# The first memory tile in two halves, and the second weight block held until it has landed

## The chip, the cores and the metric

The kernel runs on one core of a Trainium2 chip. The metric is the device time of one execution in microseconds (us). The kernel before takes 2175.76 us (median of 3 runs, 2175.23 to 2175.81).

## What is computed

The reference is a decoder trunk of two layers over 1024 tokens of width 1024, in float32, with 256 memory tokens beside them. Layer 0 mixes tokens by dilated window attention (12 heads of 64), layer 1 by a gated unit over chunks of 128. Each layer also attends into the memory with 4 heads, then applies an output projection, a layer norm, a SwiGLU feed-forward and another layer norm. What matters here is cut from it:

```python
mk, mv = jnp.split(mem @ w_mem_kv[i], 2, axis=-1)        # keys and values of the 256 memory tokens
h = x @ a_w_in[j]
q, k, v, qm = jnp.split(h, [DIL_WIDTH, 2 * DIL_WIDTH, 3 * DIL_WIDTH], axis=-1)
mo = memory_attention(qm, mk, mv)                        # first thing that the kernel works on
mix = dilated_attention(q, k, v)
y = jnp.concatenate([mix, mo], axis=-1) @ w_out[i]
```

## The kernel before, in words

Every float32 product is made of three matmuls on split operands (`three`, L359 to L363: high by high, low by high, high by low). A tile of 128 tokens is turned by 8 transposes on TensorE into PSUM (`turn_pe`, L1063), ScalarE copies the high part out (`turn_act`, L1075) and VectorE the rest (`turn_dve`, L1079). A block of weights (a "unit", 128 columns of a matrix, 512 KB, fetched as 512-byte pieces) is loaded into one of two raw slots by `load` (L235 to L243) from the SyncE queue, and GpSimd splits it into high and low (`split`, L318 and L321). `load` of unit u waits until unit u - 2 has been split (`split_done`); units 0 and 1 wait for nothing. A projection on TensorE (`proj_pe`) waits until its unit has been split.

The opening of the kernel, which is all that the change touches:

- SyncE's queue loads units in the order 0 (memory keys, from `w_mem_kv`), 1 (memory queries, from `a_w_in`), 2 (memory values), 3 (keys of the second pair of memory heads), 4, and so on.
- ScalarE's queue issues, one after the other, the identity matrix (64 KB), memory tile 0, memory tile 1 (512 KB each, 4 KB pieces), and then x in five DMAs: tile 0, tile 1, tiles 2 and 3, 4 and 5, 6 and 7 (4 MB in all). Only then does ScalarE begin to compute.
- TensorE, in its program's order: turn memory tiles 0 and 1, x tile 0, wait for the low part of memory tile 0, x tile 1, wait for the low part of memory tile 1, the key projection of unit 0 (24 matmuls of 256 columns), turn x tiles 2 to 5, the query projection of unit 1 (24 matmuls of 512 columns), turn x tiles 6 and 7, the first part of the value projection of unit 2, and then the attention stream, in which the projections of later units are interleaved. Where one of these waits, everything behind it on TensorE waits too.
- GpSimd splits the units in their order.

SyncE's DMAs are queue q1 in the profile, ScalarE's are q10. Both are served by the same 16 DMA engines.

Of the kernel before, what the change touches and what calls it, by code (L numbers as in the profile page):

```python
# [25 lines left out]
D = 1024  # L26
# [3 lines left out]
KT = D // P  # L30
# [53 lines left out]
def build(nc, a, out):  # L84
    base = -(-nc.sbuf_base // 64) * 64

    def at(name, shape, dt, off):
        return nc.alloc_sbuf_tensor_at(name, shape, dt, offset=base + off)
# [3 lines left out]
    def sem(name):  # L92
        if name not in sems:
            sems[name] = nc.alloc_semaphore(name)
        return sems[name]
# [22 lines left out]
    memraw = at("memraw", [P, 2, D], F32, A_MV + 16 * KB)  # L118
# [107 lines left out]
    def bank(b, n=512, off=0):  # L226
        return ps[:, 512 * b + off:512 * b + off + n]


    def cols(w, c0):  # L230

        return w[:, bass.ds(c0, P)].rearrange("(k p) c -> p k c", p=P)


    def load(sp, u, src):  # L235
        if not (isinstance(u, int) and u < RS):
            sp.wait_ge(split_done, u - RS + 1)
        slot = load.turn % RS
        load.turn += 1
        dst = raw[:, slot, :]  # L240
        if len(src.shape) == 3:
            dst = dst.rearrange("p (k c) -> p k c", c=P)
        sp.dma_start(dst, src).then_inc(raw_landed[slot], 16)  # L243
# [19 lines left out]
    def letters(p):  # L263

        return "qkv" if p >= NMP else "kqv"
# [200 lines left out]
    def at_(name, value=None):  # L466
        s = sem(f"att_{name}")
        return s if value is None else (s, value)
# [147 lines left out]
    def proj_pe(pe, what, g, h, k0, k1):  # L616

        u = weight_unit(g, what, h)
        n = proj_cols(g, what)
        if k0 == 0:  # L620
            pe.wait_ge(split_done, u + 1)
            if bank_user(what, g, h):
                pe.wait_ge(*evacuated(*bank_user(what, g, h)))
            if (what, g, h) == ("q", 0, 1):
                pe.wait_ge(*gi("xt_low", NT))
            if (what, g, h) == ("q", 8, 1):
                pe.wait_ge(*gf[0]("xt_low", 2 * KT))
        for k in range(k0, k1):
            wh, wl = wtile(slot_of(u), k)
            if n == M:  # L630
                xh, xl = memTh[:, k, :], memTl[:, k, :]
            else:
                xh, xl = XTh[:, k, h * 512:h * 512 + 512], XTl[:, k, h * 512:h * 512 + 512]
            mm = three(bank(proj_bank(g, what, h), n), wh, wl, xh, xl, k == 0, k == KT - 1)
        if k1 == KT:
            mm.then_inc(at_(f"{what}_proj"), 1)

    def v_turn_pe(pe, g, h):
        r = rank(g, "v", h)
        pe.wait_ge(*at_("v_copied", r + 1))  # L640
        for t in range(proj_cols(g, "v") // P):
            mm = nc.tensor.transpose(bank(proj_bank(g, "v", h), P, t * P), buf(g).vT[:, t * P:(t + 1) * P], ident[:, :])
        mm.then_inc(at_("v_turned"), 1)
# [410 lines left out]
            if L == 0 and j == len(seq):  # L1054
                out_dve(dve, 0)

    def turn_pe(pe, g, t, src, nk=KT, bb=0, after=None):

        if t >= 2:
            pe.wait_ge(*g("xt_low", t - 1 if after is None else after))  # L1060
        b = bb + 2 * (t % 2)
        for k in range(nk):
            mm = nc.tensor.transpose(bank(b + k // 4, P, (k % 4) * P), src(k), ident[:, :])  # L1063
        mm.then_inc(g("xt_turned"), 1)

    def columns(x):
        return lambda k: x[:, k * P:(k + 1) * P]
# [71 lines left out]
    def row_turn(pe, g, j, c):  # L1139
        h, k = j // KT, j % KT  # L1140
        if k == 0:
            pe.wait_ge(*g("normed", 4 * h + 4))
        if j == KT or (j == 0 and g is gf[0]):
            pe.wait_ge(*g("added", first_unit(g, c) + 8 * (h + 1 if g is gf[0] else 2) + g.credit))
        b, before = row_bank(g, j)
        if before is not None:
            pe.wait_ge(*row_read(g, before))
        for i in range(4):
            mm = nc.tensor.transpose(bank(b, P, i * P), XR[:, 4 * h + i, k * P:(k + 1) * P], ident[:, :])  # L1149
        mm.then_inc(g("row_turned"), 1)  # L1150
# [11 lines left out]
    def row_read(g, j):  # L1162

        return g("odd_high" if j % 2 else "even_high", j // 2 + 1)
# [216 lines left out]
    gm = [Names("memory", {"xt_turned": 2, "xt_high": 2, "xt_low": 2}, L) for L in range(2)]  # L1381
# [114 lines left out]
    def turn_memory_pe(pe, t):  # L1496

        if t == 0:
            pe.wait_ge(sem("mem_landed1"), 32)
            pe.wait_ge(*gf[0]("gated", 4 * NCONV + 2))  # L1500
        else:
            pe.wait_ge(*gf[0]("added", UNITS_OF_FFN - 2 + gf[0].credit))
        turn_pe(pe, gm[1], t, columns(memraw[:, 1 - t, :]), bb=1 + t)
# [213 lines left out]
    def pair_pe(pe, L, p, first=False, second=False):  # L1717
        tile_pe(pe, L, p, 0, first, second)
        tile_pe(pe, L, p, 1, first)
# [762 lines left out]
    def x_banks(t):  # L2482

        return X_BANK[t] - 2 * (t % 2)
# [6 lines left out]
    def _(sp):  # L2491
        w = [a["a_w_in"][0], a["b_w_in"][0]]

        def mem_units():
            for p in range(NMP):
                src = {"q": cols(w[0], 3 * DIL_W + p * P), "k": cols(a["w_mem_kv"][0], p * P),
                       "v": cols(a["w_mem_kv"][0], MEM_W + p * P)}
                for j in range(3):
                    load(sp, 3 * p + j, src[letters(p)[j]])

        def second_units():
# [192 lines left out]
    @block.tensor  # L2694
    def _(pe):
        pe.wait_ge(sem("const_landed"), 16)
        def turn_x(t):
            if t in X_FROM:
                pe.wait_ge(sem(f"x_landed{X_FROM.index(t)}"), 16)
            turn_pe(pe, gi, t, columns(XR[:, t, :]), bb=x_banks(t), after=X_AFTER[t])  # L2700

        def ready_first(g, i):
            if (g, i) == (0, 0):
                pe.wait_ge(*gi("xt_low", 7))
        for t in range(2):
            pe.wait_ge(sem(f"mem_tile{t}"), 16)
            turn_pe(pe, gm[0], t, columns(memraw[:, t, :]), bb=4)
        turn_x(0)
        pe.wait_ge(*gm[0]("xt_low", 1))
        turn_x(1)  # L2710
        pe.wait_ge(*gm[0]("xt_low", 2))
        proj_pe(pe, "k", 0, 0, 0, KT)
        for t in range(2, 6):
            if t == 4:
                pe.wait_ge(*at_("k_low", 2))
            turn_x(t)
        pe.wait_ge(*gi("xt_low", 4))
        proj_pe(pe, "q", 0, 0, 0, KT)
        turn_x(6)
        turn_x(7)  # L2720
        proj_pe(pe, "v", 0, 0, 0, 3)
        for L in range(2):
            if L == 0:
                attention_pe(pe, 0, ready_first)
            else:
                pe.wait_ge(*gf[0]("gated", 4 * NCONV + 2))
                proj_pe(pe, "q", 9, 0, 0, 3)
                turn_memory_pe(pe, 1)
                proj_pe(pe, "q", 9, 0, 3, 6)
                for j in (KT, KT + 1):  # L2730
                    row_turn(pe, gf[0], j, LAST)
                proj_pe(pe, "q", 9, 0, 6, KT)
                pe.wait_ge(*gm[1]("xt_low", 2))
                for j in (KT + 2, KT + 3):
                    row_turn(pe, gf[0], j, LAST)
                proj_pe(pe, "k", 8, 0, 0, KT)
                for j in (KT + 4, KT + 5):
                    row_turn(pe, gf[0], j, LAST)
                proj_pe(pe, "v", 8, 0, 0, KT)
                for j in (KT + 6, KT + 7):  # L2740
                    row_turn(pe, gf[0], j, LAST)
                v_turn_pe(pe, 8, 0)

                def ready(g, i):
                    if (g, i) == (8, 0):
                        pe.wait_ge(*row_read(gf[0], 2 * KT - 2))
                        pe.wait_ge(*row_read(gf[0], 2 * KT - 1))
                attention_pe(pe, 1, ready)
                sgu_pe(pe)

            for c in range(len(OUT_PARTS[L])):
                out_pe(pe, L, c, range(3 - L, NT) if c == 0 else range(NT))
            ffn_pe(pe, L, 0, True, False)
            pair_pe(pe, L, 0, first=True)
            pair_pe(pe, L, 1, second=True)
            with pe.Fori(2, NP - 1) as p:
                pair_pe(pe, L, p)
            pair_pe(pe, L, NP - 1)
            ffn_pe(pe, L, 1, False, True)

    @block.scalar
    def _(act):
        act.dma_start(ident[:, :], a["c_ident"]).then_inc(sem("const_landed"), 16)
        mem = a["mem"][0].rearrange("(t p) d -> p t d", p=P)
        for t in range(2):
            act.dma_start(memraw[:, t, :], mem[:, t, :]).then_inc(sem(f"mem_tile{t}"), 16)
        for i in range(X_PARTS):
            act.dma_start(XR[:, X_FROM[i]:X_FROM[i + 1], :],
                          a["x"][0, P * X_FROM[i]:P * X_FROM[i + 1], :].rearrange("(t p) d -> p t d", p=P)
# [209 lines left out]
```

## Time and profile before

| | |
|---|---|
| median of 3 runs | 2175.76 us |
| span of the profiled execution | 2173.8 us |
| TensorE matmul busy | 2143.0 us (99%) |
| VectorE busy | 1343.5 us (62%) |
| GpSimd busy | 1301.1 us (60%) |
| ScalarE busy | 929.9 us (43%) |
| granted TensorE clock, mean | 0.997 |

The span runs from the first to the last instruction of the profiled execution. No separate time of that execution is given; the median of the runs is 1.96 us above its span, which is what lies around it. In a timeline row the columns are the start and the duration in us, the engine (SPq and ACTq are the DMA-issuing sides of SyncE and ScalarE, PE is TensorE, DVE VectorE, POOL GpSimd), the line, the operation, what it writes and reads, the shape and the count, and in square brackets the idle time before it with what ended it.

### The profile page before, as it was taken

How to read it: one execution, taken by the hardware profiler on the slowest of the kernel's cores; microseconds unless marked ns; L12 is line 12 of the kernel's file. 1: busy time of each engine (PE TensorE's matmuls, PEld its weight loads, DVE VectorE, ACT ScalarE, POOL GpSimd, SP SyncE). 2: the span in 40 equal slices, each digit the busy share in tenths (PEclk: the TensorE clock that was granted, in tenths of full speed). 3: DMA queues.
4: the chain of work that ended last, by engine and by line, in shares of the span. 5: the costliest groups of instructions: out<-in, count | busy, mean ns of one | idle time of the engine just before them, and what ended most of it. 6: DMA issues, size and time to landing. Idle time of an engine off the chain costs nothing.

```text
span 2173.8 us, 32211 instructions
## 1 busy us (share of the span) xinstructions
PE 2143.0 (99%) x10960; PEld 1822.5 (84%) x10960; DVE 1343.5 (62%) x2447; ACT 929.9 (43%) x1751; POOL 1301.1 (60%) x863
## 2 busy tenths in 40 slices
PE   8999999999999999999999999999999999999997
PEld 7888888888888888888888899988878888888885
DVE  5655565655875555566547747657866555555567
ACT  5655555632533343443324753213444333333323
POOL 5221222374498777777773793424698777777764
PEclk9999999999999999999999999999999999999998
DMA  5211111142012111111131311201012111111111
GB/s 176 74 53 46 58 49 59 44 136 59 20 59 59 58 51 55 54 51 55 46 96 49 102 48 47 78 22 57 20 59 68 55 57 54 58 58 58 54 62 79
DMA packets 164701, 132.64 MB, mean 61 GB/s; under 512 B 12656, under 2 KB 148464, under 8 KB 164592
## 3 DMA queue, kind: packets, MB, share of 16 engines
q1 hardware_dynamic: 149568, 115.36, 17.6%
q10 hardware_dynamic: 15024, 15.83, 2.5%
q8 instruction: 68, 1.11, 0.2%
q14 instruction: 41, 0.34, 0.0%
HBM read 122.78 MB, written 4.19 MB: 58 GB/s over the span
## 4 chain that ended last, share of the span: by engine, by line
PE 91%; DVE 4%; POOL 3%; issue 1%; ACT 1%; DMA 0%; ACTq 0%; DVEq 0%; POOLq 0%
PE ps L361 27%; PE ps L363 27%; PE ps L362 27%; PE ps L716 3%; PE ps L744 2%; PE ps L745 2%; PE ps L703 2%; PE ps L704 1%; POOL Rl L1896 1%; PE ps L1149 1%; POOL XR L1333 1%; PE ps L1063 1%; DVE V L2418 1%; POOL raw L1918 0%; DVE T2l L1606 0%
## 5 line engine op out<-in xcount | busy, mean ns | idle before, releaser
L2102 DVE TENSOR_TENSOR XR<-XR,ps 128x512 f32<-128x512 f32 x504 | 338.8, 686 | 215.4 <-PE ps L363 215.4
L318 POOL TENSOR_TENSOR Wh<-raw,zcol 128x1024 fp32r<-128x1024 f32 x76 | 144.7, 1904 | 466.6 <-PE ps L363 389.5
L1896 POOL TENSOR_TENSOR Rl<-raw,Rh 128x512 fp32r<-128x512 f32 x216 | 285.6, 1324 | 121.4 <-ACT Rh L1740 118.9
L361 PE MATMUL ps<-XTh,Wh 128*128 128x512 f32 x608 | 248.6, 409 | 0.5 <-DVE bQl L922 0.4
L363 PE MATMUL ps<-XTh,Wl 128*128 128x512 f32 x608 | 238.2, 392 | 0.0
L362 PE MATMUL ps<-XTl,Wh 128*128 128x512 f32 x608 | 237.8, 391 | 0.0
L361 PE MATMUL ps<-XTh,Rh 128*128 128x512 f32 x576 | 224.3, 389 | 3.3 <-POOL Rl L1896 3.3
L362 PE MATMUL ps<-XTl,Rh 128*128 128x512 f32 x576 | 224.1, 389 | 0.0
L363 PE MATMUL ps<-XTh,Rl 128*128 128x512 f32 x576 | 224.1, 389 | 0.0
L1740 ACT ACTIVATE Rh<-raw 128x512 fp32r<-128x512 f32 x216 | 135.8, 630 | 167.7 <-PE ps L363 143.6
L361 PE MATMUL ps<-Wh,XTh 128*128 128x256 f32 (+1 forms) x576 | 192.0, 333 | 0.0
L363 PE MATMUL ps<-Wh,XTl 128*128 128x256 f32 (+1 forms) x576 | 190.2, 330 | 0.0
L362 PE MATMUL ps<-Wl,XTh 128*128 128x256 f32 (+1 forms) x576 | 190.2, 330 | 0.0
L321 POOL TENSOR_TENSOR Wl<-raw,Wh 128x1024 fp32r<-128x1024 f32 x76 | 183.7, 2418 | 6.0
L1941 POOL TENSOR_TENSOR DRl<-rows,DRh 128x512 fp32r<-128x512 f32 x108 | 140.6, 1303 | 72.5 <-ACT DRh L1811 72.5
L1811 ACT ACTIVATE DRh<-rows 128x512 fp32r<-128x512 f32 x108 | 68.2, 631 | 174.0 <-PE ps L363 174.0
L363 PEld LDWEIGHTS ps<-XTh,Wl 128*128 128x128 f32 x608 | 114.1, 188 | 25.5
L361 PEld LDWEIGHTS ps<-XTh,Rh 128*128 128x128 f32 x576 | 108.1, 188 | 26.6 <-POOL Rl L1896 4.2
L361 PEld LDWEIGHTS ps<-XTh,Wh 128*128 128x128 f32 x608 | 114.4, 188 | 16.4 <-issue 0.6
L362 PEld LDWEIGHTS ps<-XTl,Wh 128*128 128x128 f32 x608 | 114.8, 189 | 15.1
L363 PEld LDWEIGHTS ps<-XTh,Rl 128*128 128x128 f32 x576 | 108.1, 188 | 22.5
L362 PEld LDWEIGHTS ps<-XTl,Rh 128*128 128x128 f32 x576 | 108.1, 188 | 22.4
(302 smaller groups left out, 5572.4 us busy)
## 6 DMA issues: line engine op xcount, KB each, us to landing
raw<-in_w_up SPq DMA_DIRECT2D x44, 512.0 KB, 3.8
raw<-in_w_gate SPq DMA_DIRECT2D x72, 256.0 KB, 2.9
rows<-in_w_down SPq DMA_DIRECT2D x36, 512.0 KB, 3.7
raw<-in_a_w_in SPq DMA_DIRECT2D x20, 512.0 KB, 3.8
raw<-in_w_out SPq DMA_DIRECT2D x16, 512.0 KB, 3.7
raw<-in_b_w_in SPq DMA_DIRECT2D x15, 512.0 KB, 3.8
B<-in_c_bias SPq DMA_DIRECT2D x12, 512.0 KB, 3.7
raw<-in_w_mem_kv SPq DMA_DIRECT2D x8, 512.0 KB, 3.9
```

What stands on the lines that cost most here:

```text
L318: nc.gpsimd.tensor_tensor(high, raw[:, turn, :], zcol[:, 0:1].to_broadcast([P, UNIT]), ALU.add).then_inc(high_done, 1)
L321: nc.gpsimd.tensor_tensor(low, raw[:, turn, :], high.bitcast(F32), ALU.subtract).then_inc(split_done, 1)
L361: nc.tensor.matmul(dst, wh, xh, start=first, stop=False, skip_group_check=onto)
L362: nc.tensor.matmul(dst, wh, xl, start=False, stop=False, skip_group_check=onto)
L363: return nc.tensor.matmul(dst, wl, xh, start=False, stop=last, skip_group_check=onto)
L703: nc.tensor.matmul(bank(u % SU, nb), bf.Qh[:, hd, qt * P:(qt + 1) * P], K, start=True, stop=False)
L716: mm = nc.tensor.transpose(bank(4 + gi % 2, P, x * P), probs_of(g, 2 * s + ab, (lo + k) * P, (lo + k + 1) * P), ident[:, :])
L1740: nc.scalar.activation(Rh[(w - 1) % 4][:, :], source(w), ACT.Copy).then_inc(g("high"), 1)
L1811: nc.scalar.activation(DRh[:, (d - 1) % 2, :], right_source(d), ACT.Copy).then_inc(g("right_high"), 1)
L1896: nc.gpsimd.tensor_tensor(Rl[(w - 1) % 4][:, :], source(w), Rh[(w - 1) % 4][:, :].bitcast(F32), ALU.subtract).then_inc(gs[L]("low"), 1)
L1941: nc.gpsimd.tensor_tensor(DRl[:, (d - 1) % 2, :], right_source(d), DRh[:, (d - 1) % 2, :].bitcast(F32), ALU.subtract).then_inc(gs[L]("righ ...
L2102: nc.vector.tensor_tensor(x, x, bank(4 + i), ALU.add).then_inc(gf[L]("added"), 1)
```

## The change

Memory tile 0 is fetched as two DMAs of 128 rows by 512 columns (2 KB pieces, 256 KB each). The first half has a semaphore of its own, `mem_half0`; the second counts on `mem_tile0`. TensorE waits for the first half ahead of its first four transposes and for the second half ahead of the other four. SyncE waits for `mem_tile0` before it issues the load of unit 1; units 2 and later stand behind that in its program.

```diff
-    def turn_pe(pe, g, t, src, nk=KT, bb=0, after=None):
+    def turn_pe(pe, g, t, src, nk=KT, bb=0, after=None, half=None):
...
         for k in range(nk):
+            if half and k == KT // 2:
+                half()
             mm = nc.tensor.transpose(bank(b + k // 4, P, (k % 4) * P), src(k), ident[:, :])
...
                 for j in range(3):
+                    if (p, j) == (0, 1):
+                        sp.wait_ge(sem("mem_tile0"), 16)
                     load(sp, 3 * p + j, src[letters(p)[j]])
...
         for t in range(2):
-            pe.wait_ge(sem(f"mem_tile{t}"), 16)
-            turn_pe(pe, gm[0], t, columns(memraw[:, t, :]), bb=4)
+            if t == 0:
+                pe.wait_ge(sem("mem_half0"), 16)
+            else:
+                pe.wait_ge(sem(f"mem_tile{t}"), 16)
+            turn_pe(pe, gm[0], t, columns(memraw[:, t, :]), bb=4,
+                    half=lambda t=t: pe.wait_ge(sem(f"mem_tile{t}"), 16) if t == 0 else None)
...
         for t in range(2):
-            act.dma_start(memraw[:, t, :], mem[:, t, :]).then_inc(sem(f"mem_tile{t}"), 16)
+            for h in range(2) if t == 0 else (None,):
+                cs = slice(0, D) if h is None else slice(h * 512, h * 512 + 512)
+                act.dma_start(memraw[:, t, cs], mem[:, t, cs]).then_inc(
+                    sem("mem_half0") if (t, h) == (0, 0) else sem(f"mem_tile{t}"), 16)
```

## Rows read from the trace of the kernel before

**Rows 1.** The chain of waits that ended last, by engine, share of the span.
```profile
PE 91%; DVE 4%; POOL 3%; issue 1%; ACT 1%; DMA 0%; ACTq 0%; DVEq 0%; POOLq 0%
```
**Rows 2.** TensorE's waits, whole span: total us, times, longest us.
```profile
PE ps L1063 <- DMA memraw<-in_mem: 7.6, 1, 7.6
PE ps L361 <- POOL Rl L1896: 3.3, 2, 1.7
```
**Rows 3.** Timeline of the first 41 us, all engines.
```profile
0.82 0.43 SPq L243 DMA_DIRECT2D raw<-in_w_mem_kv  x1
...
1.31 1.24 ACTq L2766 DMA_DIRECT2D memraw<-in_mem  x2
1.32 0.58 SPq L243 DMA_DIRECT2D raw<-in_a_w_in  x1
2.57 2.48 ACTq L2768 DMA_DIRECT2D XR<-in_x  x5
...
5.19 1.89 POOL L318 TENSOR_TENSOR Wh<-raw,zcol 128x1024 fp32r<-128x1024 f32 x1 [4.28 <-DMA raw<-in_w_mem_kv]
...
7.63 3.65 PE L1063 MATMUL ps<-ident,memraw 128*128 128x128 f32 x16 [7.63 <-DMA memraw<-in_mem]
9.54 6.65 SPq L243 DMA_DIRECT2D raw<-in_w_mem_kv  x2
...
11.42 1.90 POOL L318 TENSOR_TENSOR Wh<-raw,zcol 128x1024 fp32r<-128x1024 f32 x1 [1.90 <-DMA raw<-in_a_w_in]
...
12.38 1.23 DVE L1079 TENSOR_TENSOR memTl<-ps,memTh 128x1024 fp32r<-128x1024 f32 x1 [0.48 <-ACT memTh L1075]
13.39 2.40 POOL L321 TENSOR_TENSOR Wl<-raw,Wh 128x1024 fp32r<-128x1024 f32 x1
...
13.66 0.39 PE L361 MATMUL ps<-memTh,Wh 128*128 128x256 f32 x1 [0.53 <-DVE memTl L1079]
...
20.05 1.09 PE L1063 MATMUL ps<-ident,XR 128*128 128x128 f32 x8 [0.63 <-DVE XTl L1079]
...
21.18 0.50 PE L361 MATMUL ps<-XTh,Wh 128*128 128x512 f32 x1
...
21.54 1.89 POOL L318 TENSOR_TENSOR Wh<-raw,zcol 128x1024 fp32r<-128x1024 f32 x1 [5.74 <-DMA raw<-in_w_mem_kv]
...
28.42 0.36 PE L361 MATMUL ps<-memTh,Wh 128*128 128x256 f32 x1
...
40.48 0.28 PE L361 MATMUL ps<-memTh,Wh 128*128 128x256 f32 x1
```
**Rows 4.** DMAs issued from 1.3 to 1.4 us: KB, us from issue to landing.
```profile
memraw<-in_mem ACTq DMA_DIRECT2D x1, 512.0 KB, 6.2
raw<-in_a_w_in SPq DMA_DIRECT2D x1, 512.0 KB, 10.0
```
**Rows 5.** DMA issued from 9 to 10 us.
```profile
raw<-in_w_mem_kv SPq DMA_DIRECT2D x1, 512.0 KB, 11.9
```
**Rows 6.** DMA queues, 0 to 3.5 us: packets, MB, share of 16 engines.
```profile
q1 hardware_dynamic: 491, 0.25, 24.4%
q10 hardware_dynamic: 126, 0.06, 6.1%
```
**Rows 7.** DMA queues, 4 to 5 us (q10 has no row there).
```profile
q1 hardware_dynamic: 655, 0.33, 116.0%
```
**Rows 8.** DMA queues, 5 to 6 us.
```profile
q10 hardware_dynamic: 66, 0.27, 78.9%
q1 hardware_dynamic: 151, 0.08, 31.2%
```
**Rows 9.** DMA queues, 13.2 to 20.1 us.
```profile
q10 hardware_dynamic: 616, 2.34, 86.5%
q1 hardware_dynamic: 662, 0.34, 17.1%
```
**Rows 10.** DMA queues, 20.1 to 20.8 us.
```profile
q1 hardware_dynamic: 463, 0.23, 116.8%
```

## The prediction, as made before the run

> **What bounds the kernel now.** I read the chain of waits first. The reader is to see that TensorE holds 91% of it and DMA nothing that counts [rows 1]: the time is TensorE's program, end to end, so a change matters by what it adds to or takes from TensorE's idle time. TensorE's own waits say where that is: one of 7.6 us at the start, for memory tile 0, and after it little; the next group is two waits, 3.3 us together [rows 2]. After the opening nothing has enough slack to give back a delay of TensorE, and a gain there would likewise last to the end.
>
> So I read the timeline of the opening, then the DMA landings and queues. TensorE starts at 7.63 on memory tile 0, runs 16 transposes, and begins the key projection at 13.66, released by VectorE's low part of memory tile 1 (12.38 + 1.23 = 13.61). The query projection (unit 1) starts at 21.18, right behind the last x transposes (20.05 + 1.09 = 21.14). Unit 1 landed at 1.32 + 10.0 = 11.32 [rows 4], GpSimd split it from 11.42 to 13.39 + 2.40 = 15.79 [rows 3]. So its slack is 21.18 - 15.79 = 5.4 us. That slack is what the change spends.
>
> **Why memory tile 0 is late today.** It is issued at 1.31, as unit 1 is, and lands 6.2 us later, at 7.5 [rows 3, 4]. Up to 3.5 us the queues share: q1 moved 491 packets, q10 126 (the identity) [rows 6]. From 4 to 5 us q10 has no packet at all while q1 moves 655 [rows 7]; only from 5 to 6 do 4 KB packets come on q10 [rows 8]. 491 + 655 is over the 1024 packets of unit 0, so unit 1 ran in that gap, ahead of tile 0, though q10's request was as old. I read it thus: requests of both queues are turned into descriptors in the order of their issue, one after the other. The same shows in unit 2: issued at 9.54 when q1 was almost empty, it took 11.9 us [rows 5], having the x DMAs (issued 2.57 to 5.05, [rows 3]) before it.
>
> **Part 1, unit 1 held back: what the front gains.** Without unit 1 in the way, tile 0 should start right behind the identity: about 3.6 instead of 5.0 us, 1.4 earlier. At that time unit 0 has 1024 - 491 = 533 packets left at 3.5, some 480 at 3.6, which is like the some 570 of unit 1 (2048 - 491 - 655, less what passed from 3.5 to 4) that stood beside tile 0 before. So tile 0 takes its 2.5 us as before (5.0 to 7.5) and lands at about 6.1, tile 1 about 1.4 earlier too, near 7.8 (16 transposes without a break from 7.63 put its arrival before now at no later than 9.5). The chain 16 transposes, ScalarE, VectorE then ends near 12.0, against 13.6.
>
> But the key projection also needs unit 0 split. Unit 0's last 480 packets now stand beside tile 0 and tile 1, where before they were alone. Unit 1's rest needed from 5.0 to 11.3 in that position, 6.3 us; so unit 0 lands at 3.6 + 6.3 = 9.9 at the latest, instead of about 5.1. At the earliest: tile 0 now comes in 256 packets of 2 KB, and if the engines take the queues in turn, 256 of unit 0 pass beside them until 6.1 less 0.6 for the landing; the other 224 pass at 96 per us [rows 9] in 2.3 us, and it lands at 8.4. I take 9.0, between the two. A split takes 15.79 - 11.42 = 4.37 us [rows 3], so unit 0 is ready at 13.4 (12.8 to 14.3), and the key projection starts there: 0.3 us earlier than 13.66, bounds 0.9 earlier and 0.7 later. The gain of 1.6 on the tile is mostly turned into a wait for unit 0. From there to the query projection is 21.18 - 13.66 = 7.5 us of work, so that x is ready at 20.9 (20.3 to 21.9).
>
> **Part 2, what holding back costs.** SyncE waits until about 6.1, then issues unit 1. Queued behind it in SyncE's program are unit 2 and all others; their own condition (the split of unit 0) comes at 13.4, later than that. By 6.1 all x DMAs are issued, the last at about 5.05 + 0.6 for the extra issue of a half. Unit 1 therefore takes the place that unit 2 has today: behind 4 MB of x. Unit 2's landing was 9.54 + 11.9 = 21.44. It consists of sharing (13.2 to 20.1: 662 packets in 6.9 us, 96 per us, beside x) [rows 9] and of a burst once x is over (463 in 0.7 us, 660 per us) [rows 10]. x ends 1.4 us earlier, as it starts earlier and the bytes beside it are nearly the same. So unit 1 lands at 21.44 - 1.4 = 20.0, is picked up 0.1 later (21.54 against 21.44), and is split at 20.1 + 4.4 = 24.5. The query projection starts at 24.5 instead of 21.18: **+3.3 us**.
>
> Bounds. If unit 1 isn't held behind x but flows from 1.6 us after its issue, 7.7, at 96 per us, it needs 10.7 us: 18.4 and 0.6 for the landing, 19.0, so +2.3. If tile 0 doesn't start earlier but x follows without unit 1's rest beside it (570 packets of 512 B, 0.29 MB at 2.68 MB in 6.9 us [rows 9], 0.75 us), unit 1 lands at 20.7: +4.0.
>
> **Part 3, the rest.** The first half lets TensorE start near 5.0 instead of 7.6; this is before a wait (13.4) that starts no earlier for it: nothing. One added wait on TensorE, one added issue of 0.6 us on ScalarE (1.24 for two): ScalarE is idle until its first copy at 9.6: nothing; without that cover 0.6. Unit 2 follows unit 1 by some 1.7 us (21.7), is split behind it, 24.5 to 28.9; its projection stood at 28.42 and now comes at 28.42 + 3.3 = 31.7. Unit 3 is issued at 24.5, used at 40.48 + 3.3: covered. Later units follow TensorE. Turning x 6 and 7 and the rest stay behind the query projection, so nothing regains the 3.3.
>
> **Sum.** 2173.8 + 3.3 = 2177.1 of span, with 1.96 around it: 2179.1, which is the median plus 3.3.
>
> **The clock.** The 16 transposes after the idle start took 3.65 us, 0.228 each; 8 of x at 20.05 took 1.09, 0.136 each [rows 3]. The one is the 1.2 GHz level, the other 2.4. The new idle time before the query projection is 24.5 - 20.9 = 3.6 us, longer than any after the start (1.7, [rows 2]). Should the clock fall in it, the next work loses about what the start did: 16 transposes at full pitch take some 1.9 us, so 3.65 - 1.9 = 1.7 us. The Trainium skill ("TensorE: Matmul & The Clock Gate", Part 1) says that the clock of an idle TensorE is halved and restored only after sustained activity. The trace agrees at the start; no row shows a gap as long as this one.
>
> **Rivals.**
> - The clock falls in the gap: 3.3 + 1.7 = +5.0, 2180.8. For it: the slow start. Against: the gap is half as long as that at the start, and 1.7 us gaps left no mark in the mean clock of 0.997.
> - Unit 1 arrives in time and unit 0 isn't slowed: faster. The place is the key projection, released by tile 1 at 12.0 instead of 13.66: -1.6, 2174.2. It decides if unit 1 is split by 21.18 - 1.6 = 19.6, so landed by 15.2; from 7.7 that asks for 137 packets per us against 96 measured beside x. And unit 0 would have to land by 7.6.
> - Unit 0 late, unit 1 in time: the key projection at 14.3, +0.7, 2176.5. Same objection.
> - The change doesn't do what it says: q10's gap from 4 to 5 us is a latency of ScalarE's queue, not unit 1. Then tile 0 still lands near 7, and unit 1 at 20.7: +4.0, 2179.8, within the main case's bounds.
>
> **How the numbers follow.** Main case 0.70 (2178.1 to 2179.8, of it 0.10 the last rival); falling clock 0.13; gain 0.09; unit 0 alone 0.03; nothing measurable either way 0.05. 0.2% is 4.35 us, about what tells a change from none: the line for slower is 2180.1. Slower is the falling clock and a sliver of the main case, 0.15; faster would need 2171.4, which no case gives: 0.01; the rest, 0.84, is within. The range leaves out the full gain and what is beyond the falling clock: 2176.6 to 2181.0.
>
> **What would show it.** Tile 0's first packets from 3.6 us; TensorE's first transpose near 5; unit 0's split from about 9 instead of 5.2; GpSimd's second split starting near 20.1 instead of 11.42; TensorE idle over 3 us before the 128x512 matmuls of L361, released by GpSimd (L321). If that second split starts before 16, I am wrong in the main step; if the matmuls behind the gap run at half pitch, the clock rival holds.

## The result, and the profile after

The changed kernel takes 2181.41 us (median of 8 runs, 2180.56 to 2181.87); the kernel before takes 2175.73 us beside it (8 runs, 2175.23 to 2176.35). The ratio is 1.0026, with an interval of 1.0016 to 1.0036: +5.7 us, slower. The prediction said 2179.1 with a range up to 2181.0; the time lies outside the range by 0.4 us. The span grew by 6.0 us, from 2173.8 to 2179.8.

TensorE's waits over the whole span (total us, times, longest) answer to [rows 2]:

```profile
PE ps L1065 <- DMA memraw<-in_mem: 6.3, 1, 6.3
PE ps L361 <- POOL Wl L321: 5.0, 1, 5.0
PE ps L361 <- POOL Rl L1898: 3.3, 2, 1.6
```

The wait for memory tile 0 became 1.3 us shorter, and one of 5.0 us, for GpSimd's split of unit 1, is new. The timeline of the opening answers to [rows 3]; line numbers behind the edits are higher, by 2 at first and by more for the DMAs of ScalarE:

```profile
0.82 0.43 SPq L243 DMA_DIRECT2D raw<-in_w_mem_kv  x1
...
1.30 1.57 ACTq L2776 DMA_DIRECT2D memraw<-in_mem  x3
2.90 2.78 ACTq L2779 DMA_DIRECT2D XR<-in_x  x5
5.25 1.89 POOL L318 TENSOR_TENSOR Wh<-raw,zcol 128x1024 fp32r<-128x1024 f32 x1 [4.34 <-DMA raw<-in_w_mem_kv]
...
6.26 3.68 PE L1065 MATMUL ps<-ident,memraw 128*128 128x128 f32 x16 [6.26 <-DMA memraw<-in_mem]
6.78 0.38 SPq L243 DMA_DIRECT2D raw<-in_a_w_in  x1
...
12.31 0.38 PE L361 MATMUL ps<-memTh,Wh 128*128 128x256 f32 x1 [0.49 <-DVE memTl L1081]
...
18.70 1.09 PE L1065 MATMUL ps<-ident,XR 128*128 128x128 f32 x8 [0.63 <-DVE XTl L1081]
...
20.38 1.89 POOL L318 TENSOR_TENSOR Wh<-raw,zcol 128x1024 fp32r<-128x1024 f32 x1 [10.80 <-DMA raw<-in_a_w_in]
...
22.35 2.35 POOL L321 TENSOR_TENSOR Wl<-raw,Wh 128x1024 fp32r<-128x1024 f32 x1
...
24.84 0.77 PE L361 MATMUL ps<-XTh,Wh 128*128 128x512 f32 x1 [5.05 <-POOL Wl L321]
25.40 0.63 PE L362 MATMUL ps<-XTl,Wh 128*128 128x512 f32 x1
...
29.67 0.61 PE L363 MATMUL ps<-XTh,Wl 128*128 128x512 f32 x1
30.09 0.42 PE L361 MATMUL ps<-XTh,Wh 128*128 128x512 f32 x1
30.35 0.39 PE L362 MATMUL ps<-XTl,Wh 128*128 128x512 f32 x1
...
32.85 1.91 PE L1065 MATMUL ps<-ident,XR 128*128 128x128 f32 x16
```

The 6 us can be read off it in three pieces.

1. The front gained 1.35 us: the key projection starts at 12.31 instead of 13.66, and the last x tile ahead of the query projection is turned at 18.70 + 1.09 = 19.79 instead of 21.14.
2. From there TensorE sits idle for 5.05 us, to 24.84. Unit 1 is picked up by GpSimd at 20.38 instead of 11.42. With the gain of piece 1 the query projection is 24.84 - 21.18 = 3.66 us later.
3. Its first 12 matmuls stand 0.427 us apart (25.40 to 29.67 is ten steps), the last 12 about 0.226. That is the 1.2 GHz level and then the 2.4 GHz one. The projection takes 32.85 - 24.84 = 8.01 us. Before, it took 26.75 - 21.18 = 5.57 us, since TensorE turned x tile 6 at:

```profile
26.75 1.91 PE L1063 MATMUL ps<-ident,XR 128*128 128x128 f32 x16
```

So the slow clock costs 2.4 us. The profile's record of the clock says the same. In these rows stand the stretch, its length, TensorE's busy time and matmuls in it, the granted clock as a share of 2.4 GHz, and what the DMA engines did:

```profile
22.50:23.00 0.50, 0.00 (x0) 1.00 0.00 0
23.00:23.50 0.50, 0.00 (x0) 0.81 0.00 0
29.00:30.00 1.00, 1.00 (x4) 0.50 0.00 0
30.00:31.00 1.00, 1.00 (x5) 0.93 0.65 138
```

The clock fell between 23.0 and 23.5, while TensorE was idle, and rose after 30.0, in the middle of the projection.

3.66 + 2.4 is 6.1, which is the growth of the span within 0.1 us. Nothing later gives any of it back.

### The profile page after: what moved, and what is told of

It reads as the page before. It is cut to its first block, busy times and chain, and to the rows that moved or that the text cites. A ratio compares the mean times of both kernels' runs of the same rounds, so it can differ in the third digit from the quotient of the medians.

```text
span 2179.8 us, 32212 instructions
## 1 busy us (share of the span) xinstructions
PE 2145.5 (98%) x10960; PEld 1824.4 (84%) x10960; DVE 1343.1 (62%) x2447; ACT 929.3 (43%) x1751; POOL 1300.0 (60%) x863
## 3 DMA queue, kind: packets, MB, share of 16 engines
HBM read 122.78 MB, written 4.19 MB: 58 GB/s over the span
## 4 chain that ended last, share of the span: by engine, by line
PE 91%; DVE 4%; POOL 3%; issue 1%; DMA 1%; ACT 1%; ACTq 0%; DVEq 0%; POOLq 0%
PE ps L361 27%; PE ps L363 27%; PE ps L362 26%; PE ps L716 3%; PE ps L744 2%; PE ps L745 2%; PE ps L703 2%; PE ps L704 1%; POOL Rl L1898 1%; PE ps L1151 1%; POOL XR L1335 1%; DMA raw<-in_a_w_in 1%; DVE V L2420 1%; POOL raw L1920 0%; DVE T2l L1608 0%
## 5 line engine op out<-in xcount | busy, mean ns | idle before, releaser
L361 PE MATMUL ps<-XTh,Wh 128*128 128x512 f32 x608 | 249.7, 411 | 5.5 <-POOL Wl L321 5.0
L361 PE MATMUL ps<-XTh,Rh 128*128 128x512 f32 x576 | 224.4, 390 | 3.3 <-POOL Rl L1898 3.3
L361 PE MATMUL ps<-Wh,XTh 128*128 128x256 f32 (+1 forms) x576 | 192.1, 333 | 0.0
L361 PEld LDWEIGHTS ps<-XTh,Wh 128*128 128x128 f32 x608 | 115.2, 189 | 21.6 <-DVE XTl L1081 5.3
L361 PEld LDWEIGHTS ps<-XTh,Rh 128*128 128x128 f32 x576 | 108.1, 188 | 26.4 <-POOL Rl L1898 4.1
```

The source lines that it names most:

```text
L361: nc.tensor.matmul(dst, wh, xh, start=first, stop=False, skip_group_check=onto)
```

## The experiments

Every time is compared with runs of the kernel before on the same chip, whose median was 2175.79 us for e1 to e4, 2175.74 for e5, e6, e8 and e9, and 2175.91 for f1 to f4. "Query start" is the start of the first 128x512 matmul of L361: 21.18 before, 24.84 after.

### e1 and e2: each part alone

e1 is the changed kernel without SyncE's wait; e2 is the kernel before with that wait alone.

```diff
--- e1, against the changed kernel
-                    if (p, j) == (0, 1):
-                        sp.wait_ge(sem("mem_tile0"), 16)
--- e2, against the kernel before
+                    if (p, j) == (0, 1):
+                        sp.wait_ge(sem("mem_tile0"), 16)
```

> The changed kernel with SyncE's wait taken out: only tile 0 in halves. My theory (the whole loss is unit 1 behind x and the slow clock after the idle time): unit 1 lands near 11.4 and is split by 16, no idle time before the query projection, which starts at 21.2 +- 0.3; the time is that of before within 0.5 us. If the half tiles themselves cost (smaller packets, one more issue, one more wait on TensorE), the key projection starts later than 13.66 by that cost, and up to 1 us of the 5.7 is theirs.

> The kernel before with SyncE's wait alone, tile 0 whole. My theory: unit 1 is issued near 6.8 to 7.2, lands at 20 to 20.6, the query projection starts near 25, its first 12 or so matmuls stand at 0.43 us pitch instead of 0.23, and the time is that of the changed kernel within 0.7 us (+5 to +6.4). If the halves carry a part of the loss, it is less than +5.

e1: 2175.99 us (+0.2; ratio 1.0000, 0.9991 to 1.0009), query start 21.34. e2: 2181.34 us (+5.6; ratio 1.0025, 1.0015 to 1.0034), query start 24.56, and TensorE turns x tile 6 at 32.74, as after (32.85). Timeline of e2:

```profile
6.67 0.38 SPq L243 DMA_DIRECT2D raw<-in_a_w_in  x1
6.79 3.34 PE L1063 MATMUL ps<-ident,memraw 128*128 128x128 f32 x16 [6.79 <-DMA memraw<-in_mem]
...
20.09 1.90 POOL L318 TENSOR_TENSOR Wh<-raw,zcol 128x1024 fp32r<-128x1024 f32 x1 [10.25 <-DMA raw<-in_a_w_in]
...
32.74 1.91 PE L1063 MATMUL ps<-ident,XR 128*128 128x128 f32 x16
```

The wait makes both the front's gain (in e2 TensorE is ready for the query projection at 19.98, 1.2 us earlier than before) and the whole loss. The halves alone make no difference that can be measured.

### e3 and e8: is it the idle time that lowers the clock?

Transposes of the identity, written to a free PSUM bank and read by nobody, are put ahead of the query projection: 34 in e3, 12 in e8.

```diff
+        for _ in range(34):          # 12 in e8
+            nc.tensor.transpose(bank(3, P), ident[:, :], ident[:, :])
         proj_pe(pe, "q", 0, 0, 0, KT)
```

> The changed kernel with 34 extra transposes of the identity into an unused PSUM bank right ahead of the query projection: they fill 4 us of the 5.05 us idle time and are read by nobody. My theory, that the idle time drops TensorE to its 1.2 GHz level: the query projection still starts at 24.8 but all of its matmuls stand at 0.23 us pitch; against before +3.7 instead of +5.7 to +6.1, so 2179.4. The rival, that the slow matmuls come from what runs beside them (GpSimd splitting units 1 and 2, the DMAs), expects 0.43 us pitch for some 12 of them all the same and +6.

> The changed kernel with 12 extra transposes ahead of the query projection, which are done 1.4 us after the last of x and leave about 3.6 us idle, the gap that my prediction had. My theory has no firm value: if a gap of 3.6 us is enough for the clock to fall, the time is that of the changed kernel (+5.7) and the pitch 0.43 for some 10 to 12 matmuls; if not, +3.7 as with the gap filled. Either tells whether the prediction's main case was wrong about the clock even with its own gap.

e3: 2180.07 us (+4.3; ratio 1.0020, 1.0011 to 1.0029). The extra transposes and the matmuls of L361 in e3's query projection (line, count, busy us, mean ns, idle before):

```profile
L2727 PE MATMUL ps<-ident 128*128 128x128 f32 x34 | 3.9, 274 | 0.0
L361 PE MATMUL ps<-XTh,Wh 128*128 128x512 f32 x8 | 3.2, 406 | 0.7 <-POOL Wl L321 0.7
```

and after, by the same view:

```profile
L361 PE MATMUL ps<-XTh,Wh 128*128 128x512 f32 x8 | 4.2, 529 | 5.0 <-POOL Wl L321 5.0
```

Query start is 24.71, x tile 6 is turned at 30.33: 5.62 us for the projection instead of 8.01, at the same place, beside the same splits on GpSimd and the same DMAs. The granted clock stays at 1.00 through the gap and the projection. Filling the gap took the slow matmuls away; the rival that they come from the work beside them falls.

The median gained 1.3 us rather than 2.4, and stands 0.6 above the 2179.4 expected. A part of that is the execution: the profiled one of e3 took 2179.57, 0.5 us below its median. The rest is open. Executions also differ in what the slow clock costs: in the profiles with a gap of 4.3 us or more, the projection took 7.13 us (e9), 7.16 (e5), 8.01 (after), 8.12 (e6) and 8.18 (e2), which is 1.6 to 2.6 us over the 5.57 of before.

e8: 2180.66 us (+4.9; ratio 1.0024, 1.0014 to 1.0035), with runs from 2179.67 to 2182.62, the widest spread here. In its profiled execution the gap was 3.2 us, not the 3.6 aimed at, and the clock held (granted 1.00 throughout):

```profile
L361 PE MATMUL ps<-XTh,Wh 128*128 128x512 f32 x8 | 3.2, 406 | 3.2 <-POOL Wl L321 3.2
```

Most of its loss is then the late start. The second half of memory tile 0 landed late in this execution, so unit 1 was issued at 7.58 and the query start is 25.33, 4.15 us later than before. x tile 6 is turned 4.2 us later, and the span is 5.1 us longer. Where the last 0.9 us arise was not found. The slowest run, 2182.62, has a mean granted clock of 0.996, as seven of the eight runs after the change have; the other eight runs of e8 have 0.997. So the clock may well have fallen in that one.

Of gaps seen in profiles, 3.2 us left the clock at 2.4 GHz, and 4.3 (e9), 4.6 (e2), 4.9 (e5, e6) and 5.05 us (after) dropped it to 1.2 GHz. But the length of the gap does not tell when it falls. TensorE's last work before the gap ended at 19.79 after, and the clock fell between 23.0 and 23.5. In e5 it ended at 20.01, and the clock was down from 21.5 on; in e9 it ended at 20.52, and the clock was still up at 25.0, with the projection begun. The rows of e5 and of e9:

```profile
21.50:22.00 0.50, 0.00 (x0) 0.52 0.00 0
```
```profile
24.50:25.00 0.50, 0.16 (x1) 1.00 0.00 0
25.00:26.00 1.00, 1.00 (x3) 0.51 0.15 26
```

So it fell from 1.5 to 4.5 us after the last work, and e8's one profile does not show that a gap of 3.6 us is safe.

### e4: unit 1 ahead of all of x

```diff
                     if (p, j) == (0, 1):
-                        sp.wait_ge(sem("mem_tile0"), 16)
+                        load.turn += 1
+                        continue
...
+        act.dma_start(raw[:, 1, :].rearrange("p (k c) -> p k c", c=P),
+                      cols(a["a_w_in"][0], 3 * DIL_W)).then_inc(raw_landed[1], 16)
         for i in range(X_PARTS):
```

> The changed kernel, but unit 1 is issued by ScalarE between memory tile 1 and x instead of by SyncE after tile 0 has landed. My theory, that what delays unit 1 is x standing ahead of it: it lands by 11 to 12, is split by 16, there is no idle time before the query projection, and the front's gain stays: key projection at 12.3, query projection at 19.8, time 1.0 to 1.4 below before. The rival, that a late unit 1 is late by being kept off the engines until tile 0 is through, and is as late from any queue, expects it after 15.5 and no gain.

2176.98 us (+1.2; ratio 1.0004, 0.9995 to 1.0013). Unit 1 was there at 10.66, as expected. The expected gain did not come:

```profile
10.66 1.89 POOL L318 TENSOR_TENSOR Wh<-raw,zcol 128x1024 fp32r<-128x1024 f32 x1 [0.86 <-DMA raw<-in_a_w_in]
11.90 3.67 PE L1065 MATMUL ps<-ident,XR 128*128 128x128 f32 x16 [1.07 <-DMA XR<-in_x]
...
23.11 0.50 PE L361 MATMUL ps<-XTh,Wh 128*128 128x512 f32 x1
```

x tile 0 now comes behind unit 1, at 11.9, after an idle time of 1.07 us. TensorE turns it ahead of the key projection, and the 16 transposes took 3.67 us, the pitch of the slow level; the gaps before them are a likely reason, but this was not tried. The key projection started at 15.2 and the query projection 1.9 us late, from x and not from unit 1, which had been split by 15.0.

### e5 and e6: is unit 1 late because it stands behind x?

This was the prediction's reason. e5 issues unit 1 earlier, at the identity's landing; e6 issues x tiles 4 to 7 after it.

```diff
--- e5
-                        sp.wait_ge(sem("mem_tile0"), 16)
+                        sp.wait_ge(sem("const_landed"), 16)
--- e6
-        for i in range(X_PARTS):
+        def fetch_x(i):
...
-        for t in range(2):
-            turn_act(act, gm[0], t, bb=4, high=memTh)
+        for i in range(3):
+            fetch_x(i)
+        turn_act(act, gm[0], 0, bb=4, high=memTh)
+        fetch_x(3)
+        fetch_x(4)
+        turn_act(act, gm[0], 1, bb=4, high=memTh)
```

> The changed kernel, but SyncE holds unit 1 only until the identity has landed (4.2 us) instead of tile 0's second half (6.8). At 4.2 x tiles 0, 1 and 2 to 3 are issued, x tiles 4 to 7 are not or just being issued. My theory, that descriptors of both queues are made in the order of issue: unit 1 then stands ahead of 1 to 2 MB of x, starts near 6 to 9 and lands between 13 and 17; if by 15.3, the query projection starts at 19.8 and the time is 1.3 below before; at 17 it starts at 21.5, about even. The rival, that the queues share fairly from the moment of issue, expects unit 1 from 5.8 on at some 96 packets per us, landing at 16 to 17.

> The changed kernel with SyncE's wait kept, but ScalarE issues x tiles 4 to 7 (2 MB) only after its first copy of memory tile 0 (about 9.3 us) instead of before 5.7. My theory: unit 1, issued at 6.8, has only x tiles 0 to 3 ahead of it, starts before 9 and lands near 12 to 14, so that the query projection isn't kept waiting; time 1.0 to 1.4 below before, unless x tiles 4 and 5 (then landing near 15 to 17) come late for their turn at 17.2. The rival, that the wait itself is what costs, expects unit 1 near 20 as before.

e5: 2181.72 us (+6.0; ratio 1.0027, 1.0017 to 1.0038). e6: 2181.37 us (+5.6; ratio 1.0027, 1.0017 to 1.0036). Both expectations of my theory failed. In e5 unit 1 was issued 2.6 us earlier than after, in e6 the second half of x at 8.35 instead of before 5.7, and unit 1 was picked up at 20.47 and 20.40, against 20.38 after. The rival in e5's expectation, even sharing from the issue on and a landing at 16 to 17, failed too. The DMA rows (KB, us to landing) of after, e5 and e6 in turn:

```profile
raw<-in_a_w_in SPq DMA_DIRECT2D x1, 512.0 KB, 13.5
```
```profile
raw<-in_a_w_in SPq DMA_DIRECT2D x1, 512.0 KB, 16.2
```
```profile
raw<-in_a_w_in SPq DMA_DIRECT2D x1, 512.0 KB, 13.4
```

In e5 unit 1 did begin earlier, with 9 packets between 7 and 8 us, where after there are none up to 10. It gained nothing by it. The queues show why. After, 11 to 18 us (packets, MB, share of 16 engines):

```profile
q10 hardware_dynamic: 635, 2.47, 88.1%
q1 hardware_dynamic: 637, 0.33, 15.7%
```

e5, 8 to 18 us:

```profile
q10 hardware_dynamic: 913, 3.48, 88.1%
q1 hardware_dynamic: 892, 0.46, 15.7%
```

The two queues pass the same number of packets, within 3%. One packet is 4 KB for x and 512 bytes for a weight unit, so unit 1 gets about a ninth of the bytes. Its 1024 packets outnumber those that x has left when unit 1 begins (x has 1024 in all), so it can't end before x does.

### f2: the same unit in 4 KB pieces

```diff
-                    load(sp, 3 * p + j, src[letters(p)[j]])
+                    load(sp, 3 * p + j, a["w_out"][0][0:P, :] if (p, j) == (0, 1) else src[letters(p)[j]])
```

> The changed kernel, but unit 1's load reads 128 whole rows of another matrix (w_out) in its place: the same 512 KB at the same point of the queue in pieces of 4 KB instead of 512 bytes. It leaves out the true query weights of the first pair of memory heads. The last two experiments moved unit 1's issue from 6.8 to 4.2 us, and 2 MB of x from ahead of it to behind it, and it landed at 20.3 to 20.4 all the same. My theory now: beside x a queue gets one packet for each of the other's, whatever their size, so 1024 small packets take as long as x lasts. Then 128 packets of 4 KB start near 10.8 as before and are through in some 1.5 us: unit 1 lands at 12 to 13.5, the query projection starts at 19.8 without a wait, and the time is 1.0 to 1.4 below before. The old theory, unit 1 stands behind x in the order of issue, has it land near 20 here too, and +5.7.

2174.56 us (-1.35; ratio 0.9994, 0.9985 to 1.0004; runs 2174.29 to 2175.09 against 2175.27 to 2176.54). Unit 1's DMA and the timeline:

```profile
raw<-in_w_out SPq DMA_DIRECT2D x1, 512.0 KB, 7.4
```
```profile
7.06 0.35 SPq L243 DMA_DIRECT2D raw<-in_w_out  x1
...
14.56 1.90 POOL L318 TENSOR_TENSOR Wh<-raw,zcol 128x1024 fp32r<-128x1024 f32 x1 [4.84 <-DMA raw<-in_w_out]
...
20.01 0.50 PE L361 MATMUL ps<-XTh,Wh 128*128 128x512 f32 x1
```

The queues of f2 from 12 to 13 us:

```profile
q10 hardware_dynamic: 51, 0.21, 50.8%
q1 hardware_dynamic: 51, 0.21, 50.7%
```

The wait is as after, the issue is at 7.06, and what differs is the size of the pieces and, with it, the place in memory that they are read from. The unit lands 7.4 us after its issue instead of 13.5, no wait stands before the query projection, and the front's gain is left alone: 21.18 - 20.01 = 1.2 us, and 1.35 in the medians. The interval holds 1, so the gain is not shown by it, though every run of f2 lies below every run of before; that the loss is gone is clear. Unit 1 landed at 14.5 and not at 12 to 13.5 as I expected. 51 packets per us to each queue make 2.5 us for 128, not 1.5; what else it took was not looked into.

This is shown: the loss of the change is gone when unit 1 comes in 4 KB pieces at the same point of the queue. No run reads small pieces from the other place or large ones from the old, but the packets speak for the piece size: one to one in both cases, with 51 to 51 here and 635 to 637 after.

### e9: tile 0 ahead of the identity

```diff
-        act.dma_start(ident[:, :], a["c_ident"]).then_inc(sem("const_landed"), 16)
...
+            if t == 0:
+                act.dma_start(ident[:, :], a["c_ident"]).then_inc(sem("const_landed"), 16)
```

> The changed kernel with tile 0's two halves issued ahead of the identity on ScalarE's queue. It tests the step of the prediction that failed, that unit 0's packets would stand beside tile 0's and land at 8.4 to 9.9. If descriptors are made in the order of issue and the engines then take the queues in turn, tile 0's packets start near 3.3, with over 500 of unit 0 left, unit 0 lands after 7 instead of 5.2, and the key projection is late, 13 or more. If tile 0's start is bound to the end of unit 0 (as both traces so far could also be read), or to a fixed time after its issue, unit 0 lands at 5.2 to 5.6 and the key projection starts at 12.3 or earlier. In both cases unit 1 comes near 20 and the time is that of the changed kernel within 1 us.

2180.97 us (+5.2; ratio 1.0024, 1.0015 to 1.0034). Unit 0 was picked up at 6.20 instead of 5.25, so neither at 7 or later nor at 5.2 to 5.6: it did share with tile 0 for a while, at more than one packet to one (e9, 3.5 to 4.5 us):

```profile
q1 hardware_dynamic: 294, 0.15, 49.5%
q10 hardware_dynamic: 99, 0.17, 46.4%
```

Then the identity, whose landing at 7.0 TensorE had to wait for, came late, and the key projection started at 13.03. The one-for-one of x's stretch is not what the queues do in the first microseconds. What sets the share there stays open.

### f1, f3 and f4: towards a faster version

f1 puts unit 1 on ScalarE's queue between x tile 1 and x tiles 2 and 3; f3 is the kernel before with 14 extra transposes of the identity ahead of memory tile 0; f4 is f1 with 8 of them.

```diff
--- f1 (with SyncE's load of unit 1 left out as in e4)
         for i in range(X_PARTS):
+            if i == 2:
+                act.dma_start(raw[:, 1, :].rearrange("p (k c) -> p k c", c=P),
+                              cols(a["a_w_in"][0], 3 * DIL_W)).then_inc(raw_landed[1], 16)
             act.dma_start(XR[:, X_FROM[i]:X_FROM[i + 1], :],
...
--- f3, f4
         pe.wait_ge(sem("const_landed"), 16)
+        for _ in range(14):          # 8 in f4
+            nc.tensor.transpose(bank(3, P), ident[:, :], ident[:, :])
```

> The changed kernel, but ScalarE issues unit 1 in its own queue, behind x tile 1 and ahead of x tiles 2 and 3, so that it has the engines to itself for its turn. The run with unit 1 ahead of all of x made x tile 0 late (1.1 us of wait and the clock still low, key projection at 15.5). Here x tiles 0 and 1 keep their places: key projection at 12.3; unit 1 lands at 12 to 13, split by 17.5; x tiles 4 and 5 land near 18, about when they are turned. The query projection should start at 19.9 to 20.6 against 21.18: 0.6 to 1.3 below before. If x tiles 2 to 5 come late by the whole 1.7 us of unit 1's transfer, it starts at 21 or later and nothing is gained.

> The kernel before with 14 extra transposes of the identity, read by nobody, from the identity's landing (4.2 us) to about 7.4, ahead of memory tile 0's at 7.6. If idle time is what holds TensorE at its 1.2 GHz level, the 16 transposes of the memory tiles run at 0.12 us pitch for at least a part instead of 0.228, and up to 1.7 us of the opening goes: 0.5 to 1.6 below before. If the slow opening has another cause (the first use of instructions or of memory), the 16 stay at 0.228 and the time is that of before.

> Both: unit 1 on ScalarE's queue behind x tile 1, and 8 extra transposes of the identity ahead of memory tile 0's. The warm clock saves up to 1.7 us only where transposes are what the key projection waits for; tile 1 lands at 7.7 to 8.2, so the second eight end by 8.9 instead of 9.9: the key projection at 11.3 to 12.3. 0.6 to 2.3 below before; at the most 0.2 worse than the same without the extra transposes.

f1: 2175.11 us (-0.8; ratio 0.9997, 0.9988 to 1.0006; runs 2174.93 to 2175.47). f3: 2175.43 us (-0.5; 0.9998, 0.9989 to 1.0007). f4: 2175.13 us (-0.8; 0.9997, 0.9988 to 1.0006). All three intervals hold 1, so none is shown to be faster; the profiles show where the tenths are. f1's query start is 20.66, 0.5 earlier than before. In f3 the 14 extra transposes took 3.25 us, the slow pitch, and the clock was up when tile 0 came:

```profile
7.82 1.10 PE L1063 MATMUL ps<-ident,memraw 128*128 128x128 f32 x8 [0.50 <-DMA memraw<-in_mem]
9.36 1.09 PE L1063 MATMUL ps<-ident,memraw 128*128 128x128 f32 x8 [0.44 <-DMA memraw<-in_mem]
```

Eight transposes took 1.10 us, where 16 had taken 3.65 [rows 3]; but TensorE then waits for each tile's landing, and the query projection starts at 20.73, only 0.45 earlier. The slow clock of the start was mostly hidden behind the DMAs. In f4 the 8 extra transposes were not enough: the x tiles behind were still turned at 0.23 us each, the key projection started at 13.76 where 11.3 to 12.3 was expected, and nothing came on top of f1.

One caution on the opening. The profile's granted clock reads 1.00 from 0 to 16 us in the kernels before, after, f3 and f4, also while transposes stand 0.23 us apart. There the slow level is read from the pitch alone; at the query projection pitch and granted clock agree.

## Why the prediction was wrong

**The main step held.** Holding unit 1 costs a wait at the query projection. Predicted: unit 1 lands at 20.0, query start 24.5, +3.3. Measured: 6.78 + 13.5 = 20.28, 24.84, +3.66. e2 shows that the wait alone does it.

**Its reason was wrong.** Unit 1 does not take "the place that unit 2 has today: behind 4 MB of x". e5 moved its issue ahead by 2.6 us and e6 moved 2 MB of x behind it, and it landed at the same time. f2 shows what decides: beside x as many packets of one queue pass as of the other, so 1024 small packets end only after x. I had the rate for that, 96 packets per us [rows 9], but used it for a lower bound with the unit landing at 19.0. The number came out right because both readings tie the landing to the end of x, and that is luck. The Trainium skill ("DMA: Bandwidth & Descriptors", Queues, rings and completion order) says that each engine goes round the queues it has work for at packet granularity. These traces agree beside x, 635 packets to 637; in the first microseconds of e9, 294 to 99, they don't show one for one.

**The step that failed is the clock, which the sum has at nothing.** It adds 3.3 us for the wait and no more; the falling clock stood beside it as a rival, with a chance of 0.13 and a price of 1.7 us. Measured were 3.66 us for the wait and 2.4 for the clock. So of the 2.7 us that the span grew beyond the sum, the clock made 2.4. e3 shows that the idle time lowers it. The two reasons against it did not carry. That the gap is half as long as the one at the start, and that gaps of 1.7 us left no mark, said nothing of the lengths between them. The price was too low as well: I took it from 16 short transposes of which the clock's rise may have cut some off; 12 matmuls of 512 columns at 0.427 instead of 0.226 make 2.4. And where the prediction says that the trace agrees at the start, this holds for the pitch; the granted clock reads 1.00 there.

**Part 1 failed too, and made the gap longer.** It said "Unit 0's last 480 packets now stand beside tile 0 and tile 1", with unit 0 landing at 9.0 and the key projection at 13.4. Measured: GpSimd picks unit 0 up at 5.25, nearly as before (5.19), and the key projection starts at 12.31. TensorE's first transpose comes at 6.26, not near 5. Tile 0 does not follow the identity at 3.6 us. The queues after, 4 to 5 us and 4.5 to 5.5 us:

```profile
q10 hardware_dynamic: 112, 0.22, 63.2%
q1 hardware_dynamic: 259, 0.12, 41.9%
```
```profile
q10 hardware_dynamic: 190, 0.36, 99.8%
q1 hardware_dynamic: 16, 0.01, 2.1%
```

Unit 0 is all but through before tile 0 comes in numbers. So the front's gain was whole (1.35, not 0.3). This by itself does not move the query projection, which waits for unit 1; but TensorE came to it at 19.8, not 20.9, and its gap was 5.05 us, not 3.6. Whether the clock would have held in a gap of 3.6 us is open: no profile has one, and in e5 it fell 1.5 us after the last work.

**What was right.** The halves alone cost nothing (e1), units 2 and 3 stayed covered, and no later stage regained the delay.

## What to carry to other kernels

Before a load is held back, compare its piece size with what will run beside it: beside a stream of 4 KB pieces, 512-byte pieces get as many packets and a ninth of the bytes, and issuing them a few microseconds earlier is worth nothing. A small transfer wanted soon can go into the stream's own queue, at the place where it is due (f1, query start 0.5 us earlier than before); ahead of the whole stream it makes the stream late (e4, +1.2 us). And when a wait moves onto TensorE, work out the length of the gap from its early end as well as from its late one: a gain ahead of the gap makes it longer, and behind the gaps of 4.3 to 5.05 us here a slow clock cost 1.6 to 2.6 us on top.

## What the runs showed of the hardware that I had not expected

- A DMA issued while x streamed had its first packets late: after, none of unit 1's packets ran up to 10 us, though it was issued at 6.78. e6, where the second half of x was issued behind it, shows none from 8 to 10 us either, and nor does f2 with its 4 KB pieces. In e5 it was about 3 us after the issue at 4.19. Alone, at the start, unit 0 needed 1.1 us (issued at 0.82, first packets between 1.9 and 2.0). What the delay is made of was not tried.
- The first 16 transposes behind the 7.6 us wait at the start run at the slow pitch, and taking that away (f3) moved the query projection by 0.45 us only.
- In the gap before the query projection the clock fell 1.5 us (e5), 3.2 to 3.7 us (after) and 4.5 us (e9) after TensorE's last work.
